# Sums of squares of q and k as rows on 32-column tiles, the first decays' exponentials ahead of a tanh, and a mask added to two blocks of three, in a fused two-layer decoder trunk

## The reference

```python
qkv = jax.nn.silu(causal_dwconv(qkv, conv_w))          # 4096 channels, 4 taps
q = jnp.repeat(l2norm(heads(q, 8)), 2, axis=1)         # l2norm: t * rsqrt(sum(t*t) + 1e-6)
k = jnp.repeat(l2norm(heads(k, 8)), 2, axis=1)         # 8 heads of 128
beta = sigmoid(b); g = -exp(a_log) * softplus(a + dt_bias)
# chunked gated delta rule, per v head (16 of them, two to each k head):
gc = cumsum(g)
decay = where(lower, exp(gc_i - gc_j), 0)
l_mat = where(strict, (k*beta) @ k.T * decay, 0);  attn = q @ k.T * decay
# triangular solve with (I + l_mat), then the recurrence over chunks
```

## Time and profile before

| | |
|---|---|
| median of 3 runs | 1395.39 us (1394.62 to 1398.47) |
| the profiled execution's own time | 1399.66 us |
| its span, first to last instruction | 1397.9 us |
| mean granted TensorE clock | 0.948 |
| PE busy | 1147.5 us, 82% |
| DVE busy | 402.4 us, 29% |
| ACT busy | 230.7 us, 17% |
| GDN's projections (L957), first and last start | 628.8 to 769.3 us |

### The profile page before, as it was taken

One profiled execution on the slowest core, in us unless ns is written; L12 is line 12 of the kernel. 1 busy time (PEld: TensorE's weight loads), 2 busy tenths in 40 slices (PEclk: granted clock), 3 DMA queues, 4 the chain that ended last, 5 costly groups with the idle time before them and its releaser, 6 DMA issues. The chain is left out here.

```text
span 1397.9 us, 34182 instructions
## 1 busy us (share of the span) xinstructions
PE 1147.5 (82%) x14931; PEld 727.8 (52%) x14931; DVE 402.4 (29%) x1109; ACT 230.7 (17%) x612; POOL 14.4 (1%) x29
## 2 busy tenths in 40 slices
PE   8998789977777777769899999988987777676675
PEld 4444355544444444448788558445554444444443
DVE  1254422211111111134458844133221111111113
ACT  0133201100000100023433214111111000000001
POOL 0000000000000000010000000000000000000000
PEclk9999999999999999989999999989999999999998
DMA  9933599999999999973333333589999999999993
GB/s 357 361 121 151 196 408 426 427 425 428 426 425 427 428 423 429 424 273 131 111 121 121 121 121 121 214 347 389 423 426 427 425 429 426 425 426 426 428 422 165
DMA packets 63141, 461.22 MB, mean 330 GB/s; under 512 B 3824, under 2 KB 4000, under 8 KB 30320
## 3 DMA queue, kind: packets, MB, share of 16 engines
q1 hardware_dynamic: 61680, 455.92, 79.5%
q0 software_dynamic: 1408, 4.56, 0.9%
HBM read 459.41 MB, written 1.05 MB: 329 GB/s over the span
## 5 line engine op out<-in xcount | busy, mean ns | idle before, releaser
L854 PE MATMUL bank<-ring,arena 128*32 128x128 f32 x4480 | 172.4, 314 | 111.2 <-DMA ring<-in_moe_w 97.0
L854 PEld LDWEIGHTS bank<-ring,arena 128*32 128x32 f32 x4480 | 148.7, 124 | 129.9 <-DMA ring<-in_moe_w 92.3
L854 PE MATMUL bank<-arena 128*32 128x128 f32 x3456 | 111.7, 280 | 72.0 <-DMA arena<-in_moe_w 59.6
L854 PEld LDWEIGHTS bank<-arena 128*32 128x32 f32 x3456 | 98.8, 109 | 82.5 <-DMA arena<-in_moe_w 51.6
L1187 ACT ACTIVATE arena<-bank 128x256 f32<-128x256 f32 (+3 forms) x178 | 75.0, 423 | 361.7 <-PE bank L825 138.4
L812 PE MATMUL bank<-x,pick 128*32 128x256 f32 x1024 | 130.9, 637 | 0.4 <-DVEq L1634 0.4
L1689 DVE SCALAR_TENSOR_TENSOR gated<-gated,bank 128x128 f32<-128x128 f32 x64 | 18.5, 288 | 389.6 <-ACT gated L1266 389.6
L957 PE MATMUL bank<-xy,ring 128*128 128x256 f32 x512 | 116.3, 386 | 0.0
L957 PEld LDWEIGHTS bank<-xy,ring 128*128 128x128 f32 x512 | 97.9, 194 | 13.5 <-issue 0.8
L868 PE MATMUL bank<-ring,hT 128*32 128x256 f32 x1696 | 102.5, 382 | 1.0 <-DMA ring<-in_moe_w 0.7
L1266 ACT ACTIVATE gated<-bank 128x128 f32<-128x128 f32 x64 | 17.7, 277 | 451.9 <-PE bank L854 451.9
(11 more groups left out here) (246 smaller groups left out, 979.1 us busy)
## 6 DMA issues: line engine op xcount, KB each, us to landing
ring<-in_moe_w SPq DMA_DIRECT2D x123, 2048.0 KB, 40.0
arena<-in_moe_w SPq DMA_DIRECT2D x65, 2048.0 KB, 40.5
ring<-in_gdn_w_in SPq DMA_DIRECT2D x12, 2048.0 KB, 8.9
ring<-in_ab_w_in SPq DMA_DIRECT2D x5, 2048.0 KB, 21.2
ring<-in_gdn_w_out SPq DMA_DIRECT2D x4, 2048.0 KB, 8.3
held<-in_moe_w SPq DMA_DIRECT2D x2, 2048.0 KB, 17.1
ring<-in_ab_w_out SPq DMA_DIRECT2D x2, 2048.0 KB, 24.3
xy<-in_moe_w SPq DMA_DIRECT2D x2, 2048.0 KB, 15.8
```

What stands on the lines that cost most here:

```text
L854: last = mm(psum[5][h * CAP:(h + 1) * CAP, m * FH:(m + 1) * FH], xeT[:, j], slot_tile(slots[m])[:, j, h // 2 * SEQ + h % 2:(h // 2 + 1) * ...
```

## The change: what it does

Five edits, all but one in GDN.

1. **Squares as rows.** `squares` is called four times, after the steps 3, 5, 7 and 9, each time for two finished pairs of blocks (four heads). The weights are now 32 columns of a small constant, `head_one` (a column of ones among zeros), the squares stream through as 256 columns, and each head has its own 32-column tile of the array (`tile_position`). The second call of a pair adds its four heads in the next row, by taking the 32 columns one to the left. Sums of k and q then lie as rows 0 and 1 of each 32-partition strip.
2. **Turned by transposes.** Since they are wanted with tokens on partitions, ACT takes the log of the whole 128x256 tile for k (or copies it for q) into `norm_rows`, and PE turns it with two transposes (`turn_norms`): for k in the middle of the first block of step 6, for q after step 10. ACT then copies and exponentiates 8 columns for each half of the tokens; `eps_q` is made on DVE in two instructions in step 11 in place of one in step 10.
3. **Decays ahead of the tanh.** In the steps 6 to 9, ACT runs `decays` of the first pair before the tanh and that of the second pair after it. In step 6 the log set is loaded first, and `col_bias` is corrected at the start of DVE's step 6, ahead of the SiLU.
4. **Mask on two blocks.** L986's matmul adds the mask to the blocks 0 and 2 of three, 256 columns in place of 384; the middle block was multiplied by zeros before. `ident_bf` is made by two copies in place of two copies and a memset (in the attention stage).
5. POOL makes `head_one` by three memsets at the very start.

The core of the diff:

```diff
                 def squares(...)
-                    pe.wait_ge(sq_sb, m + 1)
-                    w, at = m // 4, 2 * (m % 4)
-                    for i in range(2):
-                        for t in range(NT):
-                            u = t * GH + at + i
-                            last = mm(psum[2 + w][:, u:u + 1], sq[:, m % 2, i, t * P:(t + 1) * P], k("ones")[:, 0:1],
-                                      start=True, stop=True)
+                    pe.wait_ge(sq_sb, 4 * w + 2 * r_ + 2)
+                    for q in range(4):
+                        last = mm(psum[2 + w][q * 32:(q + 1) * 32, 0:SEQ], head_one[:, 1 - r_:33 - r_], sq[:, q // 2, q % 2],
+                                  start=(r_ == 0), stop=(r_ == 1), tile_position=(0, q * 32))
                     last.then_inc(ss_ps, 1)
+                def turn_norms(w):
+                    pe.wait_ge(nr_sb, w + 1)
+                    for t in range(NT):
+                        last = transpose(psum[2 + w][:, SEQ + t * P:SEQ + (t + 1) * P], norm_rows[w][:, t * P:(t + 1) * P], ident)
+                    last.then_inc(nr_ps, 1)
...
+                        if (n, i, j) == (6, 0, DJ // 2):
+                            turn_norms(0)
...
-                        last = mm(bank, mask_bf[:], ident_bf[:].rearrange("p x c -> p (x c)"), start=False, stop=True)
+                        last = mm(bank.rearrange("p (x c) -> p x c", x=3)[:, 0:3:2], mask_bf[:], ident_bf[:],
+                                  start=False, stop=True)
...
-                    if 2 <= n < 10:
-                        squares(n - 2)
+                    if n in (3, 5, 7, 9):
+                        squares((n - 3) // 4, (n - 3) // 2 % 2)
+                    if n == 10:
+                        turn_norms(1)
...
                 for n in range(17):
+                    if n == 6:
+                        nc.scalar.preload_act_table_set("natural_log_exp_and_others")
+                        act.wait_ge(ss_ps, 2)
+                        do(norm_rows[0], psum[2][:, 0:SEQ], ACT.Ln, bias=eps[:, 0:1]).then_inc(nr_sb, 1)
+                        act.wait_ge(nr_ps, 1)
...
+                        act.wait_ge(col_sb, 1)
+                    if 6 <= n < 10:
+                        decays(2 * (n - 6))
                     if n >= 1:
                         act.wait_ge(cv_sb, 2 * n)
...
-                    if n == 6:
+                    if 6 <= n < 10:
+                        decays(2 * (n - 6) + 1)
+                    if n == 10:
                         act.wait_ge(ss_ps, 4)
-                        do(ln_k.rearrange("p t h -> p (t h)"), psum[2][:, 0:NT * GH], ACT.Ln, bias=eps[:, 0:1]).then_inc(lnk_sb, 1)
-                        act.wait_ge(lnk_sb, 1)
-                        own.link(do(norm_k, ln_k, ACT.Exp, scale=0.5))
-                        act.wait_ge(col_sb, 1)
-                    if 6 <= n < 10:
-                        for e in range(2):
-                            decays(2 * (n - 6) + e)
+                        copy(norm_rows[1], psum[3][:, 0:SEQ]).then_inc(nr_sb, 1)
```

More of the change, by code:

```diff
@@ L224, in build @@
         mask_bf = sb("mask_bf", [P, P], BF16)
-        ident_bf = sb("ident_bf", [P, 3, P], BF16)
+        ident_bf = sb("ident_bf", [P, 2, P], BF16)
+        head_one = sb("head_one", [P, 1 + 32])
         head_bf = sb("head_bf", [P, VH], BF16)
@@ L322, in build @@
         sq = area(64, [2, 2, SEQ])
+        norm_rows = (area(68, [SEQ]), area(64, [SEQ]))
         vT = area(68, [2, 2, SEQ])
@@ L385, in build @@
                              "col_sb", "epq_sb"))
+        nr_sb, nr_ps, nk_sb = sem("nr_sb"), sem("nr_ps"), sem("nk_sb")
         cv_ps, xc_sb, cv_sb, ce_sb, si_sb, sq_sb, ss_ps, vt_ps, r_sb = (
@@ L600, in load_ln @@
                 pool.dma_start(dst[:, 1], b.partition_broadcast(P)).then_inc(ln_in, 16)
+            nc.gpsimd.memset(head_one[:, 0:1], 0.0)
+            nc.gpsimd.memset(head_one[:, 1:2], 1.0)
+            nc.gpsimd.memset(head_one[:, 2:], 0.0)
             nc.gpsimd.memset(flag[:], 0).then_inc(init, 1)
@@ L1556, in attention @@
                         own(v.tensor_copy(mask_bf[:], k("mask_a")[:, 0:P]))
-                        own(v.tensor_copy(ident_bf[:, 0], ident))
-                        own(v.memset(ident_bf[:, 1], 0.0))
-                        own(v.tensor_copy(ident_bf[:, 2], ident))
+                        for x_ in range(2):
+                            own(v.tensor_copy(ident_bf[:, x_], ident))
                         own(v.tensor_copy(head_bf[:], k("stack")[:, 0:VH]))
```

40 lines of the change are left out of this document (27 added, 13 removed).

## The result

The changed kernel takes **1386.89 us** (median of 5 runs, 1385.10 to 1390.31), against 1395.39 for the kernel before beside it: ratio 0.9941, 95% interval 0.9921 to 0.9961, 8.5 us less. When the same two kernels were timed again on another occasion, the medians were 1386.18 (6 runs) and 1397.18 (25 runs): ratio 0.9930, interval 0.9914 to 0.9946, 11 us less by the medians. The kernel before moved by 1.8 us between the two occasions and the changed one by 0.7. The profiled execution after took 1386.18 with a span of 1384.3; before it was 1399.66 and 1397.9. What follows is read inside the spans.

The account below looks back on a forecast made before the run. The last third runs at the pace of the weights' stream, which GDN's end starts; PE bounds GDN to step 9's end, then DVE. Terms sum to 11.3 us, giving 1388.4 against the profiled 1399.66 and 1384.1 against the median; range 1380 to 1390.

Parts of the forecast that it names:

- squares, the calls inside the stretch: GDN up to step 9's end: cheaper calls of squares on PE gain 4.23 us, a call taking 0.48.
- mask: GDN's `decay_rows`: 16 matmuls over 256 instead of 384 columns, 0.055 us less each, gain 0.88 us.
- step 6, the large wait: GDN step 6: PE is released 3.11 us earlier by ACT's new order, of which 2.67 is not counted elsewhere.
- clock behind it: Behind step 6's wait: with two waits of 0.4 us PE's clock stays at 2.4 GHz, gain 1.66 us.
- three small waits: GDN after step 6: PE's three waits for ACT's exponentials vanish, 0.64 us each, gain 1.92 us.
- one more DVE instruction: GDN step 11: one more small instruction on DVE's chain loses 0.1 us, estimated between 0 and 0.2.
- The rival with tiles in turn: Squares: four 32-column matmuls don't share the array, a call takes 1.74 us; result 1387.9 to 1389.1 us, chance 0.09.
- The rival by the rule: Squares: weight loads and matmuls alternate, a call takes 2.62 us; result 1392.7 us, no difference, chance 0.03.
- The slower rival: GDN: PE's clock falls to 1.2 GHz in step 6 and stays until step 10; result 1418 us, chance 0.04.
- what it saves or loses just behind that is hidden by 1.82 us: GDN behind step 9's end: DVE sets the length, so PE's wait of 1.82 us for it hides PE's changes.
- That rival: Between 788 and 943 us: something waits for a transfer begun at a fixed time; result about 1395 us, chance 0.06.

Follow-up runs that it names:

- the kernel at full width: The changed kernel with the squares' weights 128 columns wide instead of 32-column tiles; one run, 1391.37 us.
- the kernel with filling work: The kernel before with 16 needless 128x128 float32 matmuls on PE ahead of the long wait in step 6; one run, 1393.47 us.
- the one with work in step 11: The changed kernel with 7 needless 128x128 float32 matmuls on PE in step 11; one run, 1385.54 us.
- its three single parts: The kernel before with one part each: mask on two blocks, 1395.93 us; order on ACT, 1392.01 us; squares as rows, 1392.61 us.

## Why the prediction was right, and where it wasn't

The range held the result, and the mechanism was that of the forecast: the stretch with the edits gave 11.23 us of 11.4 expected. By the terms of the sum, each measured between the same events:

| term | forecast | measured | from |
|---|---|---|---|
| squares, the calls inside the stretch | 4.23 | 3.94 | 7 x 0.81 - 3 x 0.575 |
| mask | 0.88 | 0.88 | L998 to the next row 0.11, 8 x 2 of them |
| step 6, the large wait | 2.67 | 2.90 | squares to release: 9.50 before, 677.76 - 671.51 = 6.25 now; less 0.24 and 0.11 of the terms above |
| clock behind it | 1.66 | 1.66 | 6.45 before, 682.43 - 677.76 = 4.67 now, less 0.11 |
| three small waits | 1.92 | 1.92 | no idle row from 678 to 712 |
| one more DVE instruction | -0.1 | not seen | it is behind the stretch, where PE and not DVE sets the length |

They sum to 11.30, with 0.07 left against 11.23. None of the terms holds the 0.1 to 0.2 us ahead of a call on tiles.

- **Squares: mis-sized by 0.29, by the calls alone.** A call was taken at 8 x 0.060 = 0.48 from L868, and takes 0.57 to 0.58. L868's 0.060 is the mean of 32 instructions in a row; a lone group of eight also has a start and an end, which a mean over 32 hardly holds; that this is the 0.1 is likely and wasn't tested. The rival with tiles in turn expected 1.74, and the kernel at full width shows what that looks like: 1.72. The rival by the rule of the Trainium skill's page TensorE: Matmul & The Clock Gate, section "The mechanism" in Part 3 (a weight load overlaps running matmuls only when its row group differs), expected 2.62. The trace contradicts it: eight loads of 108 ns are 0.86 us alone, longer than the whole call.
- **Step 6: right within 0.25.** The log of 128x256 takes 0.47 as assumed and starts 0.02 behind the table load. The drain of 1.38 us that the Trainium skill's page ScalarE: Activation LUTs gives in "What ACT_TABLE_LOAD costs" is seen at neither switch. By the starts PE stands 0.27 at the turn (675.31 - 673.30 - 8 x 0.2175) and 0.44 at the release (677.76 - 675.58 - 8 x 0.2175; the row shows 0.28 idle), where 0.4 and 0.4 were forecast, and the two transposes take 0.27 where 0.37 was.
- **The clock: right, and shown.** 1.00 from 676 to 700, and the kernel with filling work reproduces the 1.66 on its own. The slower rival, a clock that falls in step 6 and stays, didn't come.
- **The failed step: "what it saves or loses just behind that is hidden by 1.82 us".** The prediction read the earlier trace rows as slack of PE against DVE. It isn't: 1.56 us more on PE came out as 1.55 more in the stage, with the wait unchanged. PE bounds GDN up to its last v transposes and DVE had some 0.7 us of slack, the reverse of what was said. It cost the forecast almost nothing by luck: two of its edits fall behind the stretch, and they nearly cancel. The last call of squares gains 0.81 - 0.57 = 0.24 there, which was left out as hidden, and `turn_norms(1)` costs 718.97 - 718.75 = 0.22, which was put at nothing. The stage went from 61.32 to 61.41. A saving of more than DVE's 0.7 us in this stage wasn't tested.
- **From the stretch to the end.** MoE 1 gave nothing back: its issues come 12.7 earlier, and each stage from the first unit on is as long as in the kernel before within 1.2 us, as two profiles of one kernel are. That rival is out.
- **8.5 instead of 11.3.** The two comparisons give 8.5 and 11.0 by their medians; the second interval (7.5 to 12.0 us of 1397.18) holds 11.23, the first (5.4 to 11.0 of 1395.39) ends just below it. The stages outside the edits vary by 1 to 3 us from profile to profile, the clock at GDN's start and behind the 1.82 among them, and this is as large as what is missing. So the mechanism accounts for 11.23, and why the first comparison shows 2.7 less isn't settled. Whether the changed kernel meets that fall more often than the kernel before stays open (last section).

## What to carry to other kernels

A wait on engine X is slack only if X would have been late anyway: look at what X's releasing instruction itself waited for, and if that is the waiting engine, the wait is a round trip, and everything ahead of it counts in full. Work removed ahead of a wait for another engine comes back as a longer wait, so make the other engine's order right first; here the same 0.88 us was worth half alone and all of it behind the new order. And price a wait of a few microseconds on PE with the slow work behind it: here 3.76 us of idling cost another 1.66.

## What the runs showed of the hardware

**Matmuls on four column tiles run beside each other, loads too.** Eight float32 instructions of 256 columns take 0.57 us with 32-column weights and 1.72 with 128-column weights, for the same data; the loads are 108 and 190 ns. That was expected from L868, but not measured for this form.

**The clock can fall behind a wait of 1.8 or even 1.15 us, and does not always.** Two such waits of PE stand in GDN's last part: 1.82 for DVE (L1013) and, 30 us later, about 1.15 (L1098). The first z block behind each takes 7.03 or 7.13 us at 1.00. In the changed kernel's first profile both were longer, 8.23 behind the first (in the fence for the earlier trace rows) and 8.27 behind the second, with a clock of 0.68 there:

```profile
776.00:780.00 4.00, 4.00 (x9) 1.81 (x9) 3.97 (x5) 0.00 (x0) 0.00 (x0) 0.68 0.83 320
```

The second profile of the same kernel shows it behind the first wait alone, and the kernel before behind the second alone, at 820 us:

```profile
820.00:824.00 4.00, 4.00 (x7) 1.54 (x7) 1.31 (x2) 0.00 (x0) 0.00 (x0) 0.63 0.02 4
```

One fall more costs 1.6 us, the difference of 74.69 and 73.09 in the table of the result. Not each costs the same: behind the first wait it is 1.69 in all three profiles that have it (10.34 instead of 8.65 from PE's release to the z block's end), behind the second 1.6 to 1.7 in seven and 3.2 in three (9.8 to 10.0 and 11.5 instead of 8.27). Nine profiles have the first wait. The fall behind it is in three of the four that contain the whole change (the changed kernel twice and the one with full-width weights, not the one with work in step 11), and in none of the five others (the kernel before, its three single parts and the one with filling work). That may be chance, and no run was made to tell. The fall behind the second wait is in ten of all twelve profiles, with the z block behind it between 8.27 and 9.87 us long.
